# The squared-ReLU MLP's down projection as seven-block Strassen products, its weight sums made by adding DMAs

## What is computed

```python
hn = rms_norm(h, mlp_pre_g)
ff = square(relu(hn @ w_up))            # 512 x 4096
h = h + rms_norm(ff @ w_down, mlp_post_g)
gate = sigmoid(h @ w_ple_gate + b_ple_gate)
ple = (p @ w_ple) * gate
h = h + rms_norm(ple, ple_post_g)
```

## Time and profile before

| | |
|---|---|
| median of 3 runs | 630.57 us |
| the profiled execution: span from first to last instruction | 629.5 us |
| TensorE busy | 618.7 us, 98% |
| VectorE, ScalarE, GpSimd busy | 322.8, 265.2, 63.6 us |
| MLP, TensorE's part | 226.7 us to about 580 us |
| mean granted TensorE clock | 0.997 |

### The profile page before, as it was taken

One profiled execution on the slowest core, in us unless ns is written; L12 is line 12 of the kernel. 1 busy time (PEld: TensorE's weight loads), 2 busy tenths in 40 slices (PEclk: granted clock), 3 DMA queues, 4 the chain that ended last, 5 costly groups with the idle time before them and its releaser, 6 DMA issues.

```text
span 629.5 us, 8288 instructions
## 1 busy us (share of the span) xinstructions
PE 618.7 (98%) x2994; PEld 514.5 (82%) x2994; DVE 322.8 (51%) x507; ACT 265.2 (42%) x499; POOL 63.6 (10%) x128
## 2 busy tenths in 40 slices
PE   8999999999999999999999999999999999999995
PEld 6878888888888888888888888888888888888885
DVE  5376442566555785443335533344433455338764
ACT  6654453655455754432134432143421344233532
POOL 1166342000010120000000000000000000002011
PEclk9999999999999999999999999999999999999998
DMA  8654322213000242242212232122322122323111
GB/s 311 228 198 137 114 88 68 92 43 101 1 2 34 100 142 94 99 134 100 101 67 100 96 118 91 63 100 100 133 100 100 65 92 83 129 100 134 68 67 68
DMA packets 19179, 63.90 MB, mean 102 GB/s; under 512 B 2256, under 2 KB 2640, under 8 KB 19024
## 3 DMA queue, kind: packets, MB, share of 16 engines
q1 hardware_dynamic: 17712, 58.73, 27.3%
q10 hardware_dynamic: 1440, 4.80, 2.1%
HBM read 61.42 MB, written 2.10 MB: 101 GB/s over the span
## 4 chain that ended last, share of the span: by engine, by line
PE 93%; DMA 2%; ACT 2%; SPq 1%; DVE 1%; issue 0%; POOL 0%; ACTq 0%; DVEq 0%; POOLq 0%
PE psum L1177 29%; PE psum L1182 29%; PE psum L1181 28%; PE psum L1329 3%; DMA h<-x_dram 2%; PE psum L1231 2%; PE psum L1312 2%; SPq L1146 1%; ACT junk L726 1%; PE psum L1245 1%; ACT w_hi L696 0%; SPq L1144 0%; ACT gv L767 0%; ACT L767 0%; DVE h L643 0%
## 5 line engine op out<-in xcount | busy, mean ns | idle before, releaser
L1177 PE MATMUL psum<-w_hi,mixT_hi 128*128 128x512 f32 x320 | 125.8, 393 | 0.0
L1182 PE MATMUL psum<-w_hi,mixT_lo 128*128 128x512 f32 x320 | 124.8, 390 | 0.0
L1181 PE MATMUL psum<-w_lo,mixT_hi 128*128 128x512 f32 x320 | 124.6, 389 | 0.0
L696 ACT ACTIVATE w_hi<-raw,cols 128x512 fp32r<-128x512 f32 x112 | 76.2, 716 | 87.8 <-DMA raw<-weights_dram 51.2
L326 DVE SCALAR_TENSOR_TENSOR w_lo<-raw,cols,w_hi 128x512 fp32r<-128x512 f32 x112 | 86.9, 807 | 27.6 <-ACT w_hi L696 27.6
L1177 PE MATMUL psum<-actT_hi,w_hi 128*128 128x512 f32 x256 | 99.6, 389 | 0.0
L1181 PE MATMUL psum<-actT_lo,w_hi 128*128 128x512 f32 x256 | 99.6, 389 | 0.0
L1182 PE MATMUL psum<-actT_hi,w_lo 128*128 128x512 f32 x256 | 99.6, 389 | 0.0
L1177 PE MATMUL psum<-w_hi,actT_hi 128*128 128x512 f32 (+1 forms) x232 | 90.7, 391 | 2.1 <-DVE w_lo L326 2.1
L1182 PE MATMUL psum<-w_hi,actT_lo 128*128 128x512 f32 (+1 forms) x232 | 88.9, 383 | 0.0
L1181 PE MATMUL psum<-w_lo,actT_hi 128*128 128x512 f32 (+1 forms) x232 | 88.7, 383 | 0.0
(11 more groups left out here) (118 smaller groups left out, 652.2 us busy)
## 6 DMA issues: line engine op xcount, KB each, us to landing
raw<-weights_dram SPq DMA_DIRECT2D x98, 512.0 KB, 3.2
out_dram<-h SPq DMA_DIRECT2D x7, 256.0 KB, 2.0
xT_raw<-xT_dram SPq DMA_DIRECT2D x4, 256.0 KB, 5.4
first_raw_a<-weights_dram SPq DMA_DIRECT2D x4, 256.0 KB, 4.2
first_raw_b<-weights_dram SPq DMA_DIRECT2D x4, 256.0 KB, 6.3
xT_raw<-xT_dram SPq DMA_DIRECT2D x2, 512.0 KB, 7.7
h<-x_dram SPq DMA_DIRECT2D x2, 512.0 KB, 11.5
h<-x_dram ACTq DMA_DIRECT2D x2, 512.0 KB, 8.4
```

The costliest lines, as they stand in the source:

```text
L696: nc.scalar.activation(w_hi[:, place_at, :], source, ACT.Copy, scale=gain).then_inc(slab_hi, 1)
L1177: begin = nc.tensor.matmul(out, a_hi, b_hi, start=first, stop=False)
L1181: nc.tensor.matmul(out, a_hi, b_lo, start=False, stop=False)
L1182: return nc.tensor.matmul(out, a_lo, b_hi, start=False, stop=last)
```

## The change

`w_down` is now walked in 8 steps of 512 features (`STEPS`), the up tiles in the same steps (4 tiles per step). In each of the first 7 steps the product of 512 tokens x 512 features with 512 features x 1024 columns is taken as 2 x 2 blocks (256 tokens, 256 features, 512 columns) by a Strassen scheme: 7 block products instead of 8 (`down_product`), each 2 row tiles x 2 feature tiles x 3 matmuls. The last step is plain (`down_tile`, 8 tiles of 12 matmuls).

* Sums of weight blocks: a block is 512 KB. `raw_x` takes one by a plain DMA of SyncE, and GpSimd then issues three DMAs with `accum_op=add` into the same buffer (`add_x`), one after each split that used it; `raw_o` holds the others, one of which gets a block added (`add_o`). Each of the 7 resulting weights T is split as a whole, 128 x 1024, by ScalarE (`t_split_hi`) and VectorE (`t_split_lo`), in a ring of 3.
* Sums of activation blocks: four operations of VectorE per step (`sum_e`, `sum_s3`, `sum_s2`, `sum_s4`) on `f`, the squared ReLU, which ScalarE now makes alone (`relu`, `f_square`). Each of the 7 operands A is split, 128 x 512 (ring of 4).
* Results: VectorE reads each product's two banks into `acc` (`add_product`, 14 operations per step). Several products share a bank that is read between them, so TensorE waits for `product_added` as `back` says.
* `acc` now lies where `ple` was: ScalarE writes `ple` to DRAM (2 MB) at the start of the MLP, SyncE loads it again in two parts before the gate. The clearing of `acc` is gone. No hardware loop is left in the MLP.

The host's order of the weights is unchanged (`down_in_stream` finds the blocks in it). The core of the diff:

```diff
+PRODUCTS = 7
+BANK_CHAIN, BANK_E, BANK_12, BANK_UP = 0, 2, 4, 6
+BANK_OF_PRODUCT = (BANK_CHAIN, BANK_E, BANK_CHAIN, BANK_CHAIN, BANK_CHAIN, BANK_12, BANK_E)
+BEGINS_BANK = (True, True, False, False, False, True, False)
+T_RING, A_RING = 3, 4
...
+        acc = place("acc", [P, TT, D], at=at_area)
+        t_hi = [place(f"t_hi{i}", [P, 2, W], F32R, at=at_mixed_hi + 8 * KIB * i) for i in range(T_RING)]
+        t_lo = [place(f"t_lo{i}", [P, 2, W], F32R, at=at_mixed_hi + 8 * KIB * i + 4 * KIB)
+                for i in range(T_RING)]
+        f = [place("f0", [P, 4, W], at=at_mixed_hi + 24 * KIB), place("f1", [P, 4, W], at=at_area + 16 * KIB)]
+        at_a = [at_area + 24 * KIB, at_area + 28 * KIB, at_area + 32 * KIB, at_junk]
+        a_hi = [place(f"a_hi{i}", [P, 2, W // 2], F32R, at=at_a[i]) for i in range(A_RING)]
+        a_lo = [place(f"a_lo{i}", [P, 2, W // 2], F32R, at=at_a[i] + 2 * KIB) for i in range(A_RING)]
+        a_sum = place("a_sum", [P, 2, W // 2], at=at_work)
+        raw_x = [place(f"raw_x{i}", [P, 2, W], at=at_w_hi + 24 * KIB + 4 * KIB * i) for i in range(2)]
+        raw_o = [place(f"raw_o{i}", [P, 2, W], at=at_w_lo + 24 * KIB + 4 * KIB * i) for i in range(2)]
...
+            def t_split_lo(n):
+                dve.wait_ge(t_hi_done, n + 1)
+                nc.vector.tensor_tensor(t_lo[n % T_RING][:], t_source(n), t_hi[n % T_RING][:].bitcast(F32),
+                                        ALU.subtract).then_inc(t_lo_done, 1)
...
+            def sum_e(step):
+                dve.wait_ge(f_done, 4 * step + 4)
+                nc.vector.tensor_tensor(a_sum[:], a_block(step, 1, 0), a_block(step, 1, 1), ALU.subtract
+                                        ).then_inc(a_summed, 1)
...
+            def add_product(n):
+                step, i = divmod(n, PRODUCTS)
+                second, half = ((0, 0), (1, 1), (0, 1), (1, 1), (1, 0), (0, 0), (0, 1))[i]
+                how = ALU.subtract if i in (2, 3) else ALU.add
+                for j in range(2):
+                    bank = psum[:, BANK_OF_PRODUCT[i] + j, :]
+                    part = acc[:, 2 * second + j, half * W:(half + 1) * W]
+                    if n == 0 and j == 0:
+                        dve.wait_ge(ple_spilled, 16)
+                    dve.wait_ge(product_filled, 2 * n + j + 1)
+                    if step == 0 and i == 2:
+                        nc.vector.tensor_scalar(part, bank, -1.0, None, ALU.mult).then_inc(product_added, 1)
+                    elif step == 0 and i in (0, 1, 4):
+                        nc.vector.tensor_copy(part, bank).then_inc(product_added, 1)
                     else:
-                        dve.wait_ge(filled, FILLED_FF + m + 1 + 16 * c)
-                    nc.vector.tensor_tensor(part, part, bank, ALU.add).then_inc(dve_drained, 1)
-
-            with dve.Fori(0, CHUNKS - 1) as c:
-                mlp_tiles(c, range(16))
-            last = CHUNKS - 1
-            mlp_tiles(last, range(12))
-            count[0] += 16 * CHUNKS - TT
+                        nc.vector.tensor_tensor(part, part, bank, how).then_inc(product_added, 1)
...
+            for step in range(LAST):
+                n = PRODUCTS * step
+                sum_e(step)
+                sum_s3(step)
+                if step:
+                    add_product(n - 1)
+                a_split_lo(n + 1)
+                t_split_lo(n + 2)
+                sum_s2(step)
+                a_split_lo(n + 2)
+                sum_s4(step)
+                add_product(n)
+                t_split_lo(n + 3)
+                up_lo(step + 2, 0)
+                a_split_lo(n + 3)
+                add_product(n + 1)
+                t_split_lo(n + 4)
+                add_product(n + 2)
+                up_lo(step + 2, 2)
+                t_split_lo(n + 5)
+                a_split_lo(n + 4)
+                a_split_lo(n + 5)
+                add_product(n + 3)
+                a_split_lo(n + 6)
+                t_split_lo(n + 6)
+                if step + 1 < LAST:
+                    a_split_lo(n + 7)
+                    add_product(n + 4)
+                    t_split_lo(n + 7)
+                    add_product(n + 5)
+                    up_lo(step + 2, 4)
+                    t_split_lo(n + 8)
+                    up_lo(step + 2, 6)
...
+            def t_split_hi(n):
+                step, i = divmod(n, PRODUCTS)
+                if i == 0:
+                    act.wait_ge(x_raw_loaded[step % 2], 16 * (step // 2 + 1))
+                elif i in (1, 2, 4):
+                    act.wait_ge(x_added, 16 * (3 * step + (1, 2, 0, 3)[i - 1]))
+                elif i == 3:
+                    act.wait_ge(o_added, 16 * (step + 1))
+                else:
+                    turn_o = 3 * step + i - 4
+                    act.wait_ge(o_raw_loaded[turn_o % 2], 16 * (turn_o // 2 + 1))
+                if n >= T_RING:
+                    act.wait_ge(product_filled, 2 * (n - T_RING + 1))
+                nc.scalar.activation(t_hi[n % T_RING][:], t_source(n), ACT.Copy).then_inc(t_hi_done, 1)
...
+            for step in range(LAST):
+                n = PRODUCTS * step
+                a_split_hi(n + 1)
+                t_split_hi(n + 2)
+                a_split_hi(n + 2)
+                t_split_hi(n + 3)
+                up_hi(step + 2, 0)
+                a_split_hi(n + 3)
+                relu(step + 1, 0)
+                t_split_hi(n + 4)
+                f_square(step + 1, 0)
+                up_hi(step + 2, 2)
+                t_split_hi(n + 5)
+                a_split_hi(n + 4)
+                relu(step + 1, 1)
+                a_split_hi(n + 5)
+                f_square(step + 1, 1)
+                a_split_hi(n + 6)
+                t_split_hi(n + 6)
+                if step + 1 < LAST:
+                    a_split_hi(n + 7)
+                    relu(step + 1, 2)
+                    f_square(step + 1, 2)
+                    t_split_hi(n + 7)
+                    up_hi(step + 2, 4)
+                    t_split_hi(n + 8)
+                    relu(step + 1, 3)
+                    f_square(step + 1, 3)
+                    up_hi(step + 2, 6)
...
-            pool.wait_ge(filled, filled1["ple", 7])
-            nc.gpsimd.memset(acc[:], 0.0).then_inc(acc_zeroed, 1)
+            def add_x(step, rows, half, i):
+                pool.wait_ge(t_lo_done, PRODUCTS * step + i + 1)
+                nc.gpsimd.dma_start(raw_x[step % 2][:], weights[down_in_stream(step, rows, half)],
+                                    accum_op=ALU.add).then_inc(x_added, 16)
+            def add_o(step):
+                turn_o = 3 * step
+                pool.wait_ge(o_raw_loaded[turn_o % 2], 16 * (turn_o // 2 + 1))
+                nc.gpsimd.dma_start(raw_o[turn_o % 2][:], weights[down_in_stream(step, 1, 1)],
+                                    accum_op=ALU.add).then_inc(o_added, 16)
+            add_x(0, 0, 1, 0)
+            add_o(0)
+            for step in range(LAST):
+                add_x(step, 1, 1, 1)
+                if step:
+                    add_o(step)
+                add_x(step, 1, 0, 2)
+                if step + 1 < LAST:
+                    add_x(step + 1, 0, 1, 0)
...
+            def x_raw(step, rows, half):
+                if step >= 2:
+                    sp.wait_ge(t_lo_done, PRODUCTS * (step - 2) + 5)
+                sp.dma_start(raw_x[step % 2][:], weights[down_in_stream(min(step, LAST), rows, half)]
+                             ).then_inc(x_raw_loaded[step % 2], 16)
...
+            for step in range(LAST):
+                up_pair(step + 2, 0)
+                up_pair(step + 2, 1)
+                o_raw(step, 2, 1, 1)
+                x_raw(step + 1, 0, 0)
+                if step + 1 < LAST:
+                    o_raw(step + 1, 0, 0, 1)
+                    up_pair(step + 2, 2)
+                    up_pair(step + 2, 3)
+                    o_raw(step + 1, 1, 1, 0)
...
+            def down_product(n):
+                step, i = divmod(n, PRODUCTS)
+                a, t = n % A_RING, n % T_RING
+                pe.wait_ge(t_lo_done, n + 1)
+                pe.wait_ge(a_lo_done, n + 1)
+                back = (3, 1, 2, 1, 1, 7, 5)[i]
+                for j in range(2):
+                    if n < 2 and j == 0:
+                        pe.wait_ge(*drained["before_mlp"])
+                    if n >= back:
+                        pe.wait_ge(product_added, 2 * (n - back) + j + 1)
+                    cut = slice(j * P, (j + 1) * P)
+                    for q in range(2):
+                        mm = product(psum[:, BANK_OF_PRODUCT[i] + j, :], a_hi[a][:, q, cut], a_lo[a][:, q, cut],
+                                     t_hi[t][:, q, :], t_lo[t][:, q, :], BEGINS_BANK[i] and q == 0, q == 1, read_between=True)
+                    mm.then_inc(product_filled, 1)
+            for j in range(4):
+                up_tile(0, j)
+            for step in range(LAST):
+                n = PRODUCTS * step
+                down_product(n)
+                up_tile(step + 1, 0)
```

(57 more changed lines are left out.)

416 lines of the change are left out of this document (276 added, 140 removed).

## The result

The changed kernel takes **642.28 us** (median of 4 runs, 638.86 to 645.11) where the kernel before takes 630.39 us on the same chip (4 runs, 630.18 to 631.13). The ratio is 1.0179, with a 95% interval of 1.0144 to 1.0213. Forecast were 620.5 us and faster; 642.28 lies 1.3 us above the range. The profiled execution has a span of 643.4 us, against 629.5 us before: 13.9 us more. The spans of the four are 637.1, 640.7, 640.4 and 643.4 us, with mean granted clocks of 0.991, 0.988, 0.985 and 0.980.

What follows compares the result with a forecast made beforehand. TensorE's matmuls were taken as the bound (busy 98%). The 629.5 us span less 19.1 for 84 matmuls plus 9 of stalls gave 619.4, with what lies around the span 620.5 us; range 611 to 641 us.

Steps and rivals of the forecast that it cites:

- What goes: Down projection on TensorE: 684 matmuls instead of 768, 84 fewer at 0.227 us each, 19.1 us saved if TensorE stays fed.
- Engine load: Per MLP step of 40.9 us on TensorE, VectorE has 28.4 us and ScalarE 19.7; neither becomes the bound by load.
- The chain and its place: Product 1 of steps 1 to 6 waits for VectorE's addition of product 0, behind two adding DMAs: 1.5 us each, 9 us.
- D: Time from the release of GpSimd's adding DMA to its landing: taken as 5.2 us, free up to 4.5, beyond that counted twice.
- the double load: Upper guide for an adding DMA's time: a 1024 KB load, twice the bytes of a block, took 5.8 us.
- Step 0 taken without a wait: First MLP step: its blocks are summed early and four up tiles (21.8 us) precede the first product, so no stall was counted.
- the head of the MLP without a new one: Start of the MLP: ple's 2 MB write to DRAM lands by product 1 of step 0, free, up to 2 us at risk.
- VectorE's other path: Relu, square, slabs, sums, additions and a split on VectorE and ScalarE before product 1: 10.6 us of 10.9 available, no stall.
- The clock: Rival: TensorE's granted clock falls after each MLP stall, costing 9 us more, 629.5 us in all; chance 0.07.
- rival *slower: Slow adding DMAs at product 1's wait: landing after 7 us stalls 5 us per step, 30 us, giving 641.5 us; chance 0.28.
- A step of 42.4 us: Announced sign that the forecast holds: the length of one MLP step, against 40.9 us of TensorE matmuls.
- another product waits: Announced sign that the forecast is wrong: TensorE waits at a product other than product 1, where six waits were expected.

Runs made afterwards that it cites:

- experiment 2: Changed kernel with VectorE's addition of product 0 moved ahead of the split for product 2, `back` unchanged: 618.37 us, ratio 0.9808.
- Experiments 1: Changed kernel with product 1's `back` 2 instead of 1, so it waits only for product 6's addition of the step before: 618.82 us, ratio 0.9804.
- experiment 4: Changed kernel with GpSimd's DMAs issued plainly, without their addition, so the weight sums are left out: 622.19 us, ratio 0.9865.
- experiment 7: Changed kernel with three small chained GpSimd fills before each adding DMA into `raw_x`, starting each 1.35 us later: 675.83 us, ratio 1.0723.
- experiment 3: Changed kernel with twelve useless matmuls into a free bank before product 1's wait in steps 1 to 6: 637.51 us, ratio 1.0117.

## Why the prediction was wrong, step by step

- **What goes: right.** 84 records fewer, at 0.227 us. The products' own price was not: 0.2325 in three of four places of A, 2.6 us in all. The matmuls of the earlier trace rows told only of operands in other places.
- **Engine load: right.** No engine became the bound. VectorE was busy 194 of 298 us in the change, 65%, with pauses, and 71% once they are gone (experiment 2). The 75% forecast was somewhat high; the prediction's own sum of 28.4 in 40.9 us is 69%.
- **The chain and its place: right.** Product 1, six times, released by VectorE's addition, through two adding DMAs in series. Experiments 1, 2 and 4 each cut the chain at another link and each time all six waits disappear.
- **D: mis-sized.** 5.2 was taken, 5.6 measured, within the bounds of 3.2 and 5.8. That is 0.8 us per step; another 0.3 is the rest of the list, handovers and the prediction's own rounding: a wait of 2.6 for 1.5, 15.8 us for 9. (2 x (5.2 - 4.5) is 1.4 and not 1.5, so the recorded numbers add up to 8.4 and not 9.) The row nearest to it, the double load of 5.8 us, was the better guide. The Trainium skill, DMA: Bandwidth & Descriptors (Anatomy of one DMA), with two source reads, gave an estimate of 4.4 us; the measured 5.6, with 0.3 us before the issue and an issue of 0.88, decides. For the plain load its fit gives 3.2. The row that the prediction held beside that, 3.2 us, is of loads that SyncE issued; GpSimd's own plain loads took 3.7 us in experiment 4, beside other traffic.
- **Step 0 taken without a wait, and the head of the MLP without a new one: failed.** 4.3 us. The prediction counted ple's spill, but not the bank of the first up tile, which VectorE frees only behind four weight splits, nor that product 0 of step 0 follows the last tile directly: its list of about 10 us then has only an up tile and the product, 8.2 us, to run beside. The blocks were summed early indeed; it is VectorE's other path, which the prediction had at 10.6 us but compared with 10.9 in every step.
- **The clock, put at 0 in the sum and at 0.07 in the chances: failed, and the largest single term of the profiled execution.** In the median it is an estimated 6 to 8 us, about as much as the 6.8 us by which the six waits were mis-sized. The mechanism and its size (9 us, measured 10.3) were written down, but as a rival of little weight, because the last 49.5 us of the earlier trace rows had 7 us of pauses and lost only 1.5 us. That row is a mean over a whole stretch and does not tell what stood before the fall. The fall is told by the stretches behind single pauses: in the change five of the eight pauses in the MLP are followed by the 1.2 GHz level, in experiment 7 six of six of 6.6 us or more, in experiment 3 none in the steps. The Trainium skill, TensorE: Matmul & The Clock Gate (What's actually happening), says an idle stretch brings the throttled level back; the traces agree that it can, and show that it need not.
- **Together.** In the profiled execution 6.8 (the six waits), 4.3, 10.3 and 2.6 us stand above the forecast, 24.0 in all, and 643.4 - 619.4 is 24.0. The median is 21.8 above its forecast: less of the clock, and some 0.6 us because 1.7 us lie around a span here (645.11 for 643.4), not the 1.1 of the sum. No single one turns the sign, since the forecast had 10.1 us in hand; the clock of the profiled execution alone brings it to no change, and with any other term it is a loss. The rival *slower* had the right place and side, but put all of it on D at 7, where D was 5.6.
- **The signs announced.** "A step of 42.4 us" was 43.9 (product 1 at 353.03 and 396.93); "another product waits" and "the clock falls below 1.00" were named as what would show the forecast wrong, and the clock did.

What stays open: what decides whether a short pause costs the clock, why the second adding DMA of experiment 7 is slower, and the cause behind A's place.
